# The second tile's last norm pass of an encoder block as a diagonal product onto the offset's row product on TensorE, copied out by ScalarE

## The reference

```python
def layer_norm(x, g, b):
    xf = x.astype(jnp.float32)
    mu = jnp.mean(xf, axis=-1, keepdims=True)
    var = jnp.mean(jnp.square(xf - mu), axis=-1, keepdims=True)
    y = (xf - mu) * lax.rsqrt(var + LN_EPS) * g.astype(jnp.float32) + b.astype(jnp.float32)
    return y.astype(x.dtype)
...
        f = peer_layer(x, peer_wq[i], peer_keys1[i], peer_keys2[i], peer_u[i], peer_v[i])
        e = jax.nn.sigmoid(jnp.einsum('bsd,de->bse', x, ple_gate_w[i])) * jnp.einsum('bsc,cd->bsd', p[i], ple_w[i])
        x = layer_norm(ALPHA * x + f + e, ln2_g[i], ln2_b[i])
```

## Time and profile before

| | us |
|---|---|
| median of three runs | 2285.75 |
| the profiled execution's own time | 2284.3 |
| its span, first to last instruction | 2282.4 |
| TensorE busy in the span | 2240.9 (98%) |
| VectorE busy | 1532.3 (67%) |
| ScalarE busy | 1067.6 (47%) |

### The profile page before, as it was taken

One profiled execution on the slowest core, in us unless ns is written; L12 is line 12 of the kernel. 1 busy time (PEld: TensorE's weight loads), 2 busy tenths in 40 slices (PEclk: granted clock), 3 DMA queues, 4 the chain that ended last, 5 costly groups with the idle time before them and its releaser, 6 DMA issues.

```text
span 2282.4 us, 39033 instructions
## 1 busy us (share of the span) xinstructions
PE 2240.9 (98%) x12096; PEld 1932.7 (85%) x12096; DVE 1532.3 (67%) x2818; ACT 1067.6 (47%) x1483; POOL 45.8 (2%) x93
## 2 busy tenths in 40 slices
PE   7999999999999999999999999999999999999996
PEld 5888888998888888888888888888888888888885
DVE  6457666765744599998888888887555555555556
ACT  3444555654444444445454444444444444444442
POOL 1000000000000000011000000000000000000000
PEclk9999999999999999999999999999999999999998
DMA  7555555557455556565555445555666666666653
GB/s 266 188 188 173 179 182 172 189 192 249 144 193 182 169 186 201 188 207 189 187 164 162 159 160 163 162 163 171 193 193 198 201 203 201 205 204 200 203 192 131
DMA packets 122730, 425.40 MB, mean 186 GB/s; under 512 B 13449, under 2 KB 21657, under 8 KB 121793
## 3 DMA queue, kind: packets, MB, share of 16 engines
q1 hardware_dynamic: 119040, 410.04, 56.0%
q0 software_dynamic: 3648, 14.82, 2.0%
HBM read 420.60 MB, written 6.31 MB: 187 GB/s over the span
## 4 chain that ended last, share of the span: by engine, by line
PE 87%; DVE 7%; issue 3%; DMA 2%; DVEq 1%; ACT 0%; SPq 0%; ACTq 0%
PE ps L1516 26%; PE ps L1534 25%; PE ps L1522 14%; PE ps L1541 13%; PE ps L1811 3%; DVE w_lo L846 2%; PE ps L1499 1%; PE ps L1580 1%; PE ps L1504 1%; PE ps L1500 1%; PE ps L1586 1%; DMA raw<-in_w_in 1%; DVE bn L858 0%; DMA x<-in_x 0%; DMA raw<-in_wout 0%
## 5 line engine op out<-in xcount | busy, mean ns | idle before, releaser
L846 DVE TENSOR_TENSOR w_lo<-raw,w_hi 128x1024 fp32r<-128x1024 f32 x770 | 940.9, 1223 | 452.2 <-PE ps L1541 385.3
L502 ACT ACTIVATE w_hi<-raw 128x1024 fp32r<-128x1024 f32 x770 | 815.7, 1061 | 901.8 <-DMA raw<-in_peer_v 360.3
L1516 PE MATMUL ps<-x_t_hi_lo,w_hi 128*128 128x512 f32 x3200 | 815.9, 397 | 1.2 <-DVE experts L955 1.2
L1516 PEld LDWEIGHTS ps<-x_t_hi_lo,w_hi 128*128 128x128 f32 x3200 | 574.0, 189 | 107.1 <-issue 2.7
L1534 PE MATMUL ps<-w_hi,x_t_hi_lo 128*128 128x512 f32 x2552 | 631.2, 389 | 1.3 <-DVE x_t_hi_lo L1419 1.2
L1534 PEld LDWEIGHTS ps<-w_hi,x_t_hi_lo 128*128 128x128 f32 x2552 | 478.2, 188 | 100.8 <-issue 1.9
L1522 PEld LDWEIGHTS ps<-x_t_hi_lo,w_lo 128*128 128x128 f32 x3200 | 435.0, 190 | 38.7 <-DVE w_lo L846 7.0
L1522 PE MATMUL ps<-x_t_hi_lo,w_lo 128*128 128x256 f32 x3200 | 446.7, 282 | 2.4 <-DVE w_lo L846 2.1
L1541 PE MATMUL ps<-w_lo,x_t_hi_lo 128*128 128x512 f32 x1276 | 341.2, 389 | 1.2 <-DVE w_lo L846 1.2
L1541 PEld LDWEIGHTS ps<-w_lo,x_t_hi_lo 128*128 128x128 f32 x1276 | 239.4, 188 | 51.4 <-DVE w_lo L846 1.6
L1339 DVE TENSOR_SCALAR onehots<-iota,i_t,gate_t 128x128 f32<-128x128 bf16 x256 | 77.8, 352 | 0.0
(11 more groups left out here) (218 smaller groups left out, 1134.9 us busy)
## 6 DMA issues: line engine op xcount, KB each, us to landing
raw<-in_u SPq DMA_DIRECT2D x256, 512.0 KB, 4.3
raw<-in_peer_v SPq DMA_DIRECT2D x256, 512.0 KB, 4.8
raw<-in_w_in SPq DMA_DIRECT2D x128, 512.0 KB, 4.3
raw<-in_branch SPq DMA_DIRECT2D x32, 512.0 KB, 4.1
raw<-in_wout SPq DMA_DIRECT2D x32, 512.0 KB, 4.8
raw<-in_pleg SPq DMA_DIRECT2D x32, 512.0 KB, 4.0
raw<-in_wq SPq DMA_DIRECT2D x32, 512.0 KB, 4.1
x<-in_x SPq DMA_DIRECT2D x2, 1024.0 KB, 6.6
```

The lines of the kernel that those rows point to most:

```text
L502: nc.scalar.activation(HI[:, u % 4, :], RAW[:, u % 4, :], ACT.Copy).then_inc(hi_ready, 1)
L846: v.tensor_tensor(LO[:, u % 2, :], RAW[:, u % 4, :], HI[:, u % 4, :].bitcast(F32), ALU.subtract) \
L1516: mm(PS[:, bank, :], w(HI, u % 4)[:, k, :], XHL[:, 8 * half + k, :, :].rearrange("p a t -> p (a t)"), start=(half == 0 and k == 0), stop=F ...
```

## The change

Tile 0 keeps its way, but goes second. For tile 1 the last pass (times 1/std, plus b) leaves VectorE:

- The order on VectorE is now `centre` of tile 1, `root`, a scaling of IDENT by tile 1's column of 1/std (which makes it a diagonal matrix), `centre` of tile 0, and `rescale` of tile 0 in two halves. The two halves of tile 1's `rescale` are gone.
- POOL makes the identity anew (memset and affine select) and a row of 128 ones in OH, after its last piece of the norm's constants.
- TensorE multiplies, behind its last weight product, that row of ones by the offset b, 512 columns at a time, into banks 0, 1, 4 and 5. It does so twice over: each product starts the bank afresh, so the second round writes the same again. Then it waits for the diagonal and adds diagonal x centred tile 1, four products of 512 columns. All twelve products are plain fp32.
- ScalarE copies each of the four banks out to the tile in SBUF, behind its square root.
- A memset of one column (PAD) on VectorE tells TensorE that the four banks have been read (`first_added`).
- SP issues the four stores in the order tile 1 first half, tile 0 first half, tile 1 second half, tile 0 second half; a store of tile 1 waits for two of ScalarE's copies.

```diff
@@ sync @@
-            for tt in range(NT):
-                for half in range(2):
+            for half in range(2):
+                for tt in (1, 0):
                     cols = slice(half * (D // 2), (half + 1) * (D // 2))
-                    sp.wait_ge(out_ready, 2 * tt + half + 1)
+                    if tt:
+                        sp.wait_ge(scaled_out, 2 * half + 2)
+                    else:
+                        sp.wait_ge(out_ready, half + 1)
                     sp.dma_start(out[0, tt * P:(tt + 1) * P, cols], RES2[:, tt, cols]).then_inc(out_done, 16)
@@ gpsimd, at its end @@
+            step(nc.gpsimd.memset(IDENT[:, :], 0.0))
+            nc.gpsimd.affine_select(out=IDENT[:, :], in_=IDENT[:, :], compare_op=ALU.not_equal, fill=1.0,
+                                    base=0, pattern=[[-1, P]], channel_multiplier=1).then_inc(turned_ready, 1)
+            nc.gpsimd.memset(OH[0:1, 1, 0, 0, :], 1.0).then_inc(turned_ready, 1)
@@ scalar @@
             std_of(3)
+            for q in range(4):
+                act.wait_ge(scaled_done, q + 1)
+                nc.scalar.activation(RES2[:, 1, q * 512:(q + 1) * 512], PS[:, (0, 1, 4, 5)[q], :], ACT.Copy
+                                     ).then_inc(scaled_out, 1)
@@ vector @@
+            v.memset(PAD[:, :], 0.0).then_inc(first_added, 1)
             dve.wait_ge(ln_in[2], 16 * 8)
...
             variance()
+            centre(RES2, LNG2, 1)
+            ch.wait()
+            root(3)
+            dve.wait_ge(turned_ready, 2)
+            v.tensor_scalar(IDENT[:, :], IDENT[:, :], RS[:, 1:2], None, ALU.mult).then_inc(diag_ready, 1)
             centre(RES2, LNG2, 0)
             ch.wait()
-            root(3)
             for half in range(2):
                 rescale(RES2, LNG2, 0, half, out_ready)
-            centre(RES2, LNG2, 1)
-            ch.wait()
-            for half in range(2):
-                rescale(RES2, LNG2, 1, half, out_ready)
@@ tensor, at its end @@
+            pe.wait_ge(first_added, 1)
+            pe.wait_ge(turned_ready, 2)
+            pe.wait_ge(ln_in[2], 16 * 8)
+            for again in range(2):
+                for q in range(4):
+                    mm(PS[:, (0, 1, 4, 5)[q], :], OH[0:1, 1, 0, 0, :], LNG2[0:1, 1, q * 512:(q + 1) * 512],
+                       start=True, stop=False, skip_group_check=True)
+            pe.wait_ge(diag_ready, 1)
+            for q in range(4):
+                mm(PS[:, (0, 1, 4, 5)[q], :], IDENT[:, :], RES2[:, 1, q * 512:(q + 1) * 512],
+                   start=False, stop=True, skip_group_check=True).then_inc(scaled_done, 1)
```

More of the change, by code:

```diff
@@ L294, in hybrid_block_kernel @@
         last_cols_done = sem("last_cols_done")
+        first_added = sem("first_added")
+        turned_ready = sem("turned_ready")
+        diag_ready = sem("diag_ready")
+        scaled_done = sem("scaled_done")
+        scaled_out = sem("scaled_out")
         out_ready = sem("out_ready")
```

## The result

| | before | changed |
|---|---|---|
| median, 17 runs each | 2285.8 us (2282.7 to 2288.41) | 2289.86 us (2287.42 to 2292.03) |
| ratio of the times | 1 | 1.0016, 95% interval 1.0008 to 1.0023 |
| profiled execution: its time, its span | 2284.3, 2282.4 | 2288.22, 2286.2 |

2285.4 us was forecast, with a range from 2283.6 to 2288.4. The change costs 3.7 us by the ratio.

The account below looks back on a forecast made before the run. TensorE, busy 98% of the span, was taken as the bound, with only the tail changed. Store data from 2275.95, plus 5.20 and 0.93, end the span at 2282.08 against 2282.4; 2285.75 - 0.32 gives 2285.4 us, range 2283.6 to 2288.4.

Parts of the forecast that it names:

- Up to the diagonal: VectorE's tail: 1/std there at 2272.04, the identity scaled in 0.29 us, the diagonal ready at 2272.33.
- The step that failed: TensorE's tail: eight row products at 0.86 us each, done at 2271.2, 1.1 us ahead of the diagonal, costing nothing.
- Rival C: TensorE's row products: one-row products don't count as work, clock falls at 2266.45, span ends 5.5 us later; 2291.2; chance 0.07.
- Rival B: TensorE's tail: clock falls between row and diagonal products, span ends 2.3 us later; 2288.0; chance 0.09.
- The stores: End of the tail: four stores flow without a gap for 5.20 us, from 2275.95 to 2281.15; span ends 0.93 later.
- Rival A: Stores overlap better or are not the limit: the end follows VectorE, 2.13 us earlier; 2283.6; chance in full 0.06.
- Rival D: Four stores in a row flow slower than two, 5.67 us instead of 5.20 at 370 GB/s; 2285.9; chance 0.08.

Follow-up runs that it names:

- 128 rows: The changed kernel with its eight row products taken over 128 rows in place of one; ratio to before 0.9999 (0.9990 to 1.0008).
- one round of 128 rows: The changed kernel with row products over 128 rows, made once (four instead of eight); ratio to before 1.0002 (0.9992 to 1.0011).
- zeros: The kernel with row products over 128 rows, but 127 rows of the stationary matrix hold zero; ratio to before 1.0001 (0.9991 to 1.0010).
- tile 0 first: The kernel with row products over 128 rows, but both halves of tile 0 stored before tile 1's; ratio to before 1.0002 (0.9992 to 1.0011).
- one round of either kind: Two runs of the changed kernel with four row products instead of eight: over one row, ratio 1.0009; over 128 rows, ratio 1.0002.

## Why the prediction was wrong

**Up to the diagonal it was right.** PAD's memset cost 0.02 instead of 0.06: from the last weight product's start to the next statistics are 1.24 us now and were 1.22. The scaling of the identity took 0.29, VectorE's end came at 12.99 for 13.04.

**The step that failed** is "The eight row products run from about 2264.3 to 2264.3 + 6.9 = 2271.2 ... They are 1.1 us ahead of the diagonal and so cost nothing." The number of 0.86 us a product is right at 2.4 GHz (128 rows: 7.03 for eight), and so is 1.71 at 1.2. Wrong was that the clock would stay. In the traces with one-row products it falls 2.6 to 4.4 us behind the last product of 128 rows; where TensorE stood still instead, it was 2.0 us (before) and 3.2 (one round of 128 rows). These ranges overlap: one-row products did not hold the clock any more than standing still did, while the profile counts them as busy.

The price has two parts, read from the changed kernel against the one with 128 rows. The row products end late, so the diagonal products start at 9.9 instead of 8.3: 1.6 us. And up to the second copy these take 4.4 us from their start instead of 2.6: 1.8 us. Together 3.4, which is the difference of the first stores (14.38 - 10.96) and of the tails (21.34 - 17.88 = 3.46).

**Rival C was the right mechanism** and got 0.07. It read: "products of one row don't count as work, and the clock falls at 2266.45 as it did before", and gave 2291.2 where 2289.86 came. It was 1.3 us too long, because the clock held for another 1.2 to 2.4 us and came back during the diagonal products. What I set against it was that "TensorE is busy in time all along". That was no evidence, for the trace of before has no row of one-row products at the higher clock to show what they do to it. A case that no row excludes and that costs 5.5 us deserved more than 0.07, and the range should have reached to it. Rival B, a fall in the wait between row and diagonal products, is what the run with one round of 128 rows shows, where that wait is 4.4 us; with 1.0 us of it the clock held in all three traces that have it (128 rows, zeros, tile 0 first).

**The stores were right**, and they are why there was little to win. In the seven traces whose four stores flow as one (changed twice, 128 rows, zeros, one round of either kind, tile 0 first) the span ends 6.89 to 6.96 us after the first store is issued, for 6.94 forecast. Rival A (the end follows VectorE) falls with the run that stored tile 0 first. Rival D (four in a row are slower) falls too: 401 and 407 GB/s over 5 and 4 us, as a pair had the earlier trace rows. The limit of about 358 GB/s that the Trainium skill names (DMA: Bandwidth & Descriptors, Specifications) did not show for these stores either.

**Had the clock been held**, the change would have gained 18.33 - 17.88 = 0.45 us by these two traces, where 0.3 was forecast, although VectorE ends 2.2 us earlier. The ratio of the kernel with 128 rows, 0.9999 with an interval from 0.9990 to 1.0008, can't tell that from nothing.

## What to carry to other kernels

If products are there to keep TensorE's clock up, don't count on ones of a single row. In these runs only products over all 128 rows held it, those with 127 rows of zeros as well, and only when they reached to 1.0 us before the work that needed it, not to 4.4 us before. The profile's busy column does not tell, so read the granted clock beside it, and check it against what a product takes. At the start of before the clock column says 1.00 (from 14 to 16 us in the earlier trace rows, and from 19 to 23 as well), yet seven products of L1580 take 3.33 us, where eight take 1.98 at the end. Where transfers at the end already run one behind the other, only the first one's issue moves the end: work that finishes earlier behind it is worth nothing. And in a long program whose main part scatters by some us, measure an edit of the tail from the last event ahead of it, not by the total.

## What the runs showed that I had not expected

- One-row products kept TensorE busy in the profile for 9.6 and 10.8 us, and the clock fell 4.4 and 3.2 us after the last full product.
- A stationary matrix with 127 rows of zeros held the clock as well as a full one, for 7.0 us of row products and 3.7 of diagonal products.
- The clock came back to 2.4 GHz under the four plain fp32 diagonal products, at different times for the same work: 3.0 us after their start with one round, 2.8 and 5.1 in the two traces of the changed kernel, 5.6 with one round of 128 rows.
- In one trace the last two of the stores' 576 packets came late, and the end of the span with them: 1.85 us behind the stream instead of 0.93.
